# Thirty-two more tokens scored by gathered u rows, and gate work shared anew, in a one-core transformer block with a PEER layer

## What is computed

```python
def peer_ffn(h, wq, sub_keys, u, v):
    ...
        q = jnp.einsum('td,de->te', xc, wq).reshape(PEER_CHUNK, PEER_HEADS, 2, PEER_QDIM // 2)
        s = jnp.einsum('thpd,hpnd->thpn', q, sub_keys).astype(jnp.float32)
        sv, si = lax.top_k(s, PEER_TOPK)
        cand = (sv[:, :, 0, :, None] + sv[:, :, 1, None, :]).reshape(PEER_CHUNK, PEER_HEADS, -1)
        cidx = (si[:, :, 0, :, None] * PEER_NKEYS + si[:, :, 1, None, :]).reshape(PEER_CHUNK, PEER_HEADS, -1)
        top, pos = lax.top_k(cand, PEER_TOPK)
        eidx = jnp.take_along_axis(cidx, pos, axis=-1)
        g = jax.nn.softmax(top, axis=-1)
        ue = u[eidx]
        ve = v[eidx]
        a = jax.nn.gelu(jnp.einsum('thkd,td->thk', ue, xc).astype(jnp.float32), approximate=False)
        return jnp.einsum('thk,thkd->td', (g * a).astype(ve.dtype), ve)
...
    x = x + g2 * peer_ffn(h, peer_wq[l], peer_keys[l], peer_u[l], peer_v[l])
    return rmsnorm(x, final_g)
```

## Time and profile before

| | before |
|---|---|
| device time, three runs | 1567.66, 1567.62, 1569.81 us; median 1567.66 |
| profiled execution: span | 1565.4 us |
| its device time | not listed apart; the median lies 2.3 us above the span |
| PE busy | 1527.4 us, 98% |
| DVE, ACT, POOL busy | 1337.7, 660.1, 487.5 us |
| DMA | 398.77 MB, mean 255 GB/s |
| granted TensorE clock | full from 43.8 us to the end |

### The profile page before, as it was taken

How to read it: one execution, slowest core, us unless ns; L and a number is a source line. 1 busy time by engine, 2 the same in 40 slices (tenths; PEclk the granted TensorE clock), 3 DMA queues, 4 the chain that set the end, 5 groups by cost and what they waited for, 6 DMA issues and landing times.

```text
span 1565.4 us, 24588 instructions
## 1 busy us (share of the span) xinstructions
PE 1527.4 (98%) x8275; PEld 1363.9 (87%) x8275; DVE 1337.7 (85%) x2877; ACT 660.1 (42%) x1143; POOL 487.5 (31%) x450
## 2 busy tenths in 40 slices
...
GB/s 366 270 174 148 148 68 0 55 95 82 118 169 180 194 230 199 229 248 251 298 393 330 350 340 343 346 337 371 372 378 372 368 345 355 376 350 352 241 244 104
DMA packets 160467, 398.77 MB, mean 255 GB/s; under 512 B 11753, under 2 KB 75369, under 8 KB 158705
## 3 DMA queue, kind: packets, MB, share of 16 engines
...
## 4 chain that ended last, share of the span: by engine, by line
PE 83%; DVE 13%; DMA 1%; ACT 1%; issue 1%; ACTq 0%; DVEq 0%; SPq 0%
PE bank_S L907 16%; PE bank_T L907 11%; PE bank_O L858 6%; PE bank_O L856 6%; PE bank_O L857 6%; PE bank_T L885 5%; PE bank_G L907 5%; PE bank_S L856 3%; PE bank_S L857 3%; PE bank_S L858 3%; PE bank_O L643 2%; PE bank_S L610 2%; DVE mod_acc L1909 1%; DVE v_sb L1902 1%; DVE v_sb L1915 1%; DVE si L1921 1%
## 5 line engine op out<-in xcount | busy, mean ns | idle before, releaser
L1462 ACT ACTIVATE v_hi<-v_raw 128x1024 fp32r<-128x1024 f32 x124 | 131.7, 1062 | 333.9 <-PE bank_G L907 330.9
L1434 ACT ACTIVATE u_hi<-u_raw 128x1024 fp32r<-128x1024 f32 x128 | 135.9, 1061 | 243.0 <-PE bank_O L858 122.8
L1213 POOL COPY stage<-eidx 128x1 uint32<-128x1 uint32 (+1 forms) x128 | 75.7, 591 | 461.8 <-DVE eidx L2030 207.7
L1217 POOL DMA_INDIRECT row<-in_peer_u,stage x128 | 148.1, 1157 | 103.8 <-POOL stage L1213 103.8
L856 PE MATMUL bank_S<-h_hi,u_hi 128*128 128x384 f32 x512 | 179.7, 351 | 0.5 <-DVE u_lo L2002 0.5
L858 PE MATMUL bank_O<-h_hi,u_lo 128*128 128x384 f32 x512 | 171.9, 336 | 0.0
L856 PE MATMUL bank_O<-h_hi,u_hi 128*128 128x384 f32 x512 | 171.7, 335 | 0.0
L858 PE MATMUL bank_S<-h_hi,u_lo 128*128 128x384 f32 x512 | 171.5, 335 | 0.0
L857 PE MATMUL bank_O<-h_lo,u_hi 128*128 128x384 f32 x512 | 171.5, 335 | 0.0
L857 PE MATMUL bank_S<-h_lo,u_hi 128*128 128x384 f32 x512 | 171.4, 335 | 0.0
L2098 DVE SCALAR_TENSOR_TENSOR y<-row,wgt,y 128x1024 f32<-128x1024 f32 x128 | 165.9, 1296 | 0.0
(11 more groups left out here) (370 smaller groups left out, 3647.8 us busy)
## 6 DMA issues: line engine op xcount, KB each, us to landing
u_raw<-in_u_t SPq DMA_DIRECT2D x128, 512.0 KB
v_raw<-in_peer_v SPq DMA_DIRECT2D x128, 512.0 KB
gates<-g_out ACTq DMA_DIRECT2D x12, 2048.0 KB, 6.8
...
ada_late<-in_w_ada SPq DMA_DIRECT2D x8, 2048.0 KB, 8.4
spill<-a_act ACTq DMA_DIRECT2D x56, 192.0 KB, 2.1
...
```

The source lines that it names most:

```text
L1217: pool.indirect_dma_start(rows[slot][:, :], None, table[:, :], bass.IndirectOffsetOnAxis(stage[:, place:place + 1], 0))\
L1434: act.activation(u_hi[c % 2][:, :], u_raw[:, c % 2, :], ACT.Copy).then_inc(s_uhi, 1)
L1462: act.activation(v_hi_end[:, i % TAIL, :] if end else v_hi[:, c % 2, :], v_raw[c % 4][:, :], ACT.Copy)\
```

## The change

1. **32 tokens leave the dense u pass.** The last 32 tokens of tile 3 (the "X tokens", `XT`) are cut from `a_chunk`, which now has 352 columns (`DX`). Their 32 x 128 dot products come from gathered u rows, four expert places of the 32 tokens side by side on the 128 partitions: 32 indirect DMAs (`gather_x`, 512 KB each) into five places, and 32 instructions `x_dot` on DVE. 21 of these stand in the gaps (`DOTS_AFTER`), 11 beside the gate blocks (`DOTS_BESIDE`, one after the sixth group of each block but the last). Gelu times gate of these tokens enters their gate table itself, so their block, number 11, is made last, in a phase of its own. `v_chunk` still has all 384 tokens.
2. **72 early chunks, 64 spilled**, so 7 wide turns and 9 late ones. The gaps are 25, 7, 7, 5 and then 4 chunks; the phases hold 3, 4, 4 and 1 blocks, tile 3's first three ahead.
3. **Splits beside gate blocks go to POOL** (`LOW_ON_POOL`): 28 of them, two for each block and one just before each phase.
4. **`hot_j` reads its iota from PSUM** (`iota_p`, a copy); `hot_i` still reads `iota_k` in SBUF.
5. **w by pairs**: the product for two chunks at a time, into the gates' own place, a chunk ahead; `w_hi` on ACT (`w_high`); `w_lo` by pairs on DVE.
6. **The gates' layout in DRAM** puts 4 chunks of a partition together: a load reads 6144 bytes a partition where it was 12 pieces of 512, a store writes pieces of 512. SP issues the stores of a block that isn't its phase's last, two chunks later; a phase's last block is stored in quarters by ACT through the gap behind it. The spill's layout follows.
7. **Row pairs**: 12 a turn in turns 0 to 3, 14 in 4 to 6, then 5, 5, 5, 5, 5, 5, 4, 4 in turns 7 to 14. A dot overwrites its own row. Tile 0's final steps move to chunks 121 to 125.
8. The first top-k group is split in two (`sc_first`), so DVE starts on head 0 once its own two key matrices are multiplied.

```diff
-SPILL = 56
+SPILL = 64
...
+XT = 32
+DX = DT - XT
...
+PHASES = [[8, 9, 10], [0, 1, 2, 3], [4, 5, 6, 7], [X_BLOCK]]
+GAPS = [25, 7, 7, 5]
...
+LOW_ON_POOL = set(range(FIRST_LOW)) | {i for p, blocks in enumerate(PHASES)
+                                       for i in range(BESIDE[blocks[0]], BETWEEN[p + 1].start + 1)}
+DOTS_AFTER = {23: 2, 24: 3, 32: 2, 33: 2, 34: 1, 35: 1, 36: 1, 47: 1, 48: 2, 49: 1, 50: 2, 51: 1, 52: 2}
+DOTS_BESIDE = 1
...
+WIDE_ROWS = {4: 14, 5: 14, 6: 14}
+LATE_TURNS = {7: 5, 8: 5, 9: 5, 10: 5, 11: 5, 12: 5, 13: 4, 14: 4}
...
-                    pe.matmul(ps[:, 0:DT], u_lo[q][:, kk], h_hi[:, GT:NT, k, :], ...)
+                    pe.matmul(ps[:, 0:DX], u_lo[q][:, k, :], h_hi[:, k, GT * P:S - XT], ...)
...
@@ SP: load_g and the gate stores
-                    sp.dma_start(g_in[:, parity, :, :, :].rearrange("p b i t -> p b (i t)"),
-                                 gates[:, :, bass.ds(chunk_of(4 * q, late), 4), :].rearrange("b p i t -> p b (i t)"))\
+                    sp.dma_start(g_in[parity][:, :, :, :].rearrange("p b i t -> p (b i t)"),
+                                 gates[:, bass.ds(own, 1), :, :, :].rearrange("p o b i t -> p (o b i t)"))\
...
@@ POOL: the order in the early stage
+            gather_x(0, got)
+            for phase, blocks in enumerate(PHASES):
+                for i in range(BESIDE[blocks[0]], BETWEEN[phase + 1].start + 1):
+                    ready = dots_before(i) + X_PLACES
+                    gather_x(got, ready)
+                    got = max(got, ready)
+                    split_u(i, i)
...
@@ ACT: a gap of the early stage
+                for n, i in enumerate(gap):
                     u_high(i + 2, i + 2)
                     early_gelu(i)
+                    while stored < 4 and (stored + 1) * len(gap) <= 4 * (n + 1):
+                        store_quarter(blocks[-1], stored)
+                        stored += 1
...
-            act.wait_ge(s_gst[1], 16 * (BLOCKS // 2))
+            act.wait_ge(s_gst[1], 16 * stores_of(BLOCKS - 1))
+            w_high(0, 0)
...
@@ DVE: a gate block
-                    dve.tensor_tensor(hot_j[:, B % 2, :, :], iota_k[:, :].unsqueeze(1).to_broadcast([P, 4, P]),
+                        dve.tensor_tensor(hot_j[:, B % 2, :, :], iota_p.unsqueeze(1).to_broadcast([P, 4, P]),
...
-                    if B % 4 == 3:
-                        split_u(BETWEEN[tile].stop + B // 4 - 8 * tile + 1)
+                        if b == 5 and tb != X_BLOCK:
+                            for _ in range(DOTS_BESIDE):
+                                x_dot()
...
@@ DVE: the main loop
-                weigh(i, c, late)
+                if c % 2 == 0:
+                    w_low(i, c)
+                else:
+                    product(i + 1, c + 1)
```

More of the change, by code:

```diff
@@ L362, in over, with last_of_phase, stores_of, dots_before @@
             return i // n if isinstance(i, int) else (i - c) // n + c // n
-        BETWEEN = [range(0, 24), range(32, 36), range(44, 52), range(60, 64)]
-        FIRST_LOW = 17
         GATES_AT, NUMBERS_AT = 17, 12
-        def beside(tb):
-            return BETWEEN[tb // 4].stop + 2 * (tb % 4)
+        def last_of_phase(tb):
+            return any(tb == blocks[-1] for blocks in PHASES)
+        def stores_of(o):
+            return sum(4 if last_of_phase(tb) else 1 for tb, n in PLACE_OF.items() if n <= o and n % 2 == o % 2)
+        def dots_before(i):
+            dots = sum(n for a, n in DOTS_AFTER.items() if a < i)
+            return dots + sum(DOTS_BESIDE for tb, a in BESIDE.items() if tb != X_BLOCK and a + 1 < i)
         tally = {}
@@ L1463, in v_high, with w_high @@
                    .then_inc(s_vhi, 1)
+            def w_high(i, c):
+                if not within(i):
+                    return
+                if at_end(i):
+                    act.wait_ge(s_acc, PH * TOPK)
+                else:
+                    after(act, s_yv, i - 2)
+                act.wait_ge(s_pw, over(i, c, 2) + 1)
+                act.activation(weight_pair(w_hi, w_hi_end, i, c), gate_pair(c), ACT.Copy).then_inc(s_whi, 1)
             def gelu(i, slot, c):
@@ L1942, in _ @@
                     ins.then_inc(s_scu, 1)
                     dve.wait_ge(s_scu, n + 1)
[L1944 to L1948 removed]
+                else:
+                    done(dve, ins, s_dv)
@@ L1950, in decode_all @@
+            for g in range(1, 4):
+                for i in range(NT):
+                    emptied(dve, ("sc", g, i))
+                    choose(g, i, 2 * g, 2)
             def decode_all():
@@ L2065, in _, with product @@
+            for i in list(BETWEEN[-1][1:]) + [EARLY]:
                 split_u(i)
-            done(dve, dve.memset(y0[:, :], 0.0), s_dv)
+            done(dve, dve.memset(y0, 0.0), s_dv)
             dve.wait_ge(s_gm, DT // 4)
-            def weigh(i, c, late):
-                dve.wait_ge(s_g[(c // 4) % 2], 16 * (over(i, c, 8) + 1))
+            def product(i, c):
+                if not within(i):
+                    return
+                late = isinstance(i, int) and i >= MAIN
+                dve.wait_ge(s_g[c // 4 % 2], 16 * (over(i, c, 8) + 1))
```

498 lines of the change are left out of this document (330 added, 168 removed).

## The result

The changed kernel takes 1636.84 us (median of four runs, 1629.20 to 1639.17) against 1567.64: a ratio of 1.043, 95% interval 1.0405 to 1.0455. The direction was forecast, the size wasn't: +69 us instead of +18, beyond the range's end at 1596. Each time is the median of a kernel's fast runs, without one of e13's eleven that took 3813 us. The profiled execution took 1639.17 us, its span is 1637.3, 71.9 above that of before.

A forecast was written before the change was run, and what follows sets the result against it. PE was taken as the bound (83% of the chain of waits, DVE 13%), tied with DVE in the early stage. Terms: -41.0 + 46.8 + 2.5 + 8.5 + 1.0 = +17.8, so 1585.5 us against 1567.66, range 1533 to 1596.

The forecast's parts named there:

- Term 1: Dense u matmuls on PE: 32 columns fewer in 3072 matmuls, -41.0 us if nothing else sets the pace.
- Term 2: Gate blocks: hot_i stands still during POOL's splits, 2.2 us each, so DVE sets the pace: +46.8 us.
- R1: Gate blocks: hot_i runs on while POOL splits, so PE sets the pace; 1537 us in all, chance 0.32.
- R3: Gate blocks: POOL's hold is partial, a split costs DVE about 1.3 us; 1566 us in all, chance 0.08.
- break-even: Gate blocks and gaps: the sign of the whole change turns where a split costs DVE 1.5 us.
- Term 3: Gaps: DVE's decode, dots and splits slightly exceed PE's chunks, +2.5 us (0 to 6); first gap 0.
- Term 4: Turn to the main loop: PE waits for the last gate store and the load behind it, +8.5 us.
- Term 5: Main loop's DMAs: turns need 386 and 381 GB/s where 370 and 361 were seen, +1 us (0 to 8).
- R2: Main loop: as R1, but 370 GB/s is a ceiling and the DMAs set the pace; 1555 us, chance 0.07.
- DVE's dots waiting for gathered rows: DVE's dots, five places for rows: an unpriced example of something no term names that could set the end.

The follow-up runs named there:

- e13: e12 with gaps of 26, 7, 7, 4 and 4 chunks and no dots in the first gap: 1567.60 us, 0.9992 of the kernel before.
- e1: The kernel before with only the dense u matmuls cut from 384 to 354 columns: 1537.05 us, 0.9801.
- e2: The changed kernel with hot_i reading its iota from PSUM, POOL's splits untouched: 1584.53 us, 1.011 of the kernel before.
- e3: The changed kernel with the 28 splits beside gate blocks back on DVE: 1582.97 us, 1.0093 of the kernel before.
- e5: e3 without the 32 gathers of u rows, the dots multiplying h2x with itself: 1568.38 us, 1.0006 of the kernel before.
- e7: e3 with the 5 dots of the first gap moved to later gaps: 1576.22 us, 1.0047 of the kernel before.
- e12: e11 with POOL splitting the first 19 chunks of u instead of 17: 1570.56 us, 1.0017 of the kernel before.
- e11: e3 with the edits of e7 and e8, gaps of 27, 6, 6, 5 and 4 chunks, three dots after chunk 26: 1570.42 us, 1.0012.
- e4: The changed kernel with the last gate block's four quarters stored at once right after the block: 1631.22 us, 1.0404 of the kernel before.
- e8: e3 with the last gate block's four quarters stored at once right after the block: 1575.40 us, 1.0049 of the kernel before.
- e6: e3 with the gate table laid out in DRAM as before, loads in pieces of 512 bytes: 1587.25 us, 1.0118 of the kernel before.

## Why the prediction was wrong, step by step

**Term 1** (-41.0): right. e1 shows 30.9 of 38.4 arriving with nothing else changed. In the early stage only 6 of 19 us arrived, beside a DVE that is full there, and the main loop gave 5 us more than the term.

**Term 2** (+46.8): the mechanism was right and the size too small, +64.8. What the splits did to `hot_i` was forecast as 2.2 us each; it is 2.1, and 2.7 with a gather ahead, which I had left to POOL's own time. The larger omission is PE's clock: I let PE lose only the time that it waited, and behind the longer pause of a block it lost about 1.6 us more at the lower level, 1.4 of which DVE waited for. The rival R1 falls with e2 and e3: POOL's split does hold a `hot_i` that reads SBUF, and doesn't hold one that reads PSUM. R3, a partial hold of 1.3 us, falls with the 2.1. Two sums of the rivals don't come out of their own terms: break-even is at 26 x s - 4.4 + 1 = 31.5, a split at 1.3 us and not 1.5, and R3's adds up to 1562 at most, not 1566. The Trainium skill's rule (SBUF — State Buffer, "Who interferes with whom"), that a tensor_scalar in a two-port mode waits for GpSimd's whole instruction, agrees with 3.22 us in place of 1.10, and with e2.

**Term 3** (+2.5): this is the step that failed; the gaps cost 38.5. I summed DVE's work in a gap against PE's and took the loads for granted; the sum was 26.7 against 26.9, and the gap takes 34.8. The first gap I put at 0, and it is 24.5 of the 38.5 (27.5 over, 3.0 before). Three things were missing. The gathered rows and the stores share the DMA engines with the u rows, and in e3 those land in 6.0 us where PE needs them every 3.84 (e5: 7 us in the two gaps of 7, and ACT's wait down by 40). The first row is fetched only after the decode, and DVE waited 6.6 us for it with the split of the next chunk behind (e5 and e7: 7.0 us each in the first gap). And the first phase began 21.5 us later in all, 3.8 of it for one chunk more: top-k ended at 475.0 us where it had ended at 471.35, 1.6 of which the stage's later start explains, so point 8 of the change shows no gain; and a gather with two splits of POOL right behind it held its first four `hot_i` for 5.1 us:

```profile
523.08 6.21 DVE L2320 TENSOR_SCALAR hot_i<-iota_k,cols 128x128 f32<-128x128 f32 x4
```

Of the 13.8 us over that remain in the first gap without dots (e7), 4.7 lie in chunks 16 and 17, where PE waits for DVE's first split behind top-k and then runs at the lower clock; in the changed kernel it is 6.0, 3.0 of them the wait. But e12 took these away, on top of e11, and gained nothing, so what counts is when DVE comes to the first gate block, and how the time until then divides between top-k, decode and the splits stays open.

**Term 4** (+8.5): 9.5 in the trace of the changed kernel. The store's last quarter was issued at 880.79, the load at 884.71, and it had landed by SP's next issue at 888.79; I had 3.3 and 4.3 for 3.9 and 4.1. (The estimate of 3.8 us for the load was worked out from a rule for transfers that POOL issues; this one is SP's.) Of the 9.5, 7.9 are PE's pause, and the rest is the lower clock behind it: the first two v matmuls take 1.19 us where they took 0.63.

```profile
880.79 0.38 ACTq L1688 DMA_DIRECT2D gates<-g_out  x1
...
884.71 0.33 SPq L1215 DMA_DIRECT2D g_in<-gates  x1
...
891.94 1.19 PE L1027 MATMUL bank_S<-v_hi,w_hi 128*128 128x512 f32 x2 [7.76 <-DVE w_lo L2354]
```

But its price was not what removing it gives: by the stages e4 kept 2 of 9 us and e8 4.5, the rest went to ACT behind its own stores; by the medians they are 5.6 and 7.6 faster.

**Term 5** (+1): -1.2. R2's ceiling of 370 GB/s isn't one: the changed kernel moves 389 to 395 at a share of 1.00. The reason that was given against R2, that longer packets cost less, isn't shown: e6 moves 392 with pieces of 512 bytes.

The forecast's own range, 1573 to 1597, took in the bounds of term 2 but gave the gaps 6 us at most; no case had the gaps and the clock in it. The prediction named "DVE's dots waiting for gathered rows" among what would make it wrong, without a price. It should have had one: the gathered rows have 31.8% of the DMA engines' time in the changed kernel's second gap, 44% in the middle of e3's.
